# Sums of squares in four column tiles of TensorE, added by a copy and a second product

## The reference

```python
def rmsnorm(x, g):
    xf = x.astype(jnp.float32)
    xf = xf * lax.rsqrt(jnp.mean(xf * xf, axis=-1, keepdims=True) + EPS)
    return (xf * g.astype(jnp.float32)).astype(x.dtype)

mod = jax.nn.silu(cond) @ p['ada_w'][l] + p['ada_b'][l]
m = jnp.split(mod[:, None, :], 9, axis=-1)
h = rmsnorm(x, p['norm_pre'][l, n]) * (1 + m[3 * n + 1]) + m[3 * n]
y = sub_layer(h)
x = x + m[3 * n + 2] * rmsnorm(y, p['norm_post'][l, n])    # times 0.5 in the feed-forward blocks
```

## Time and profile before

| | us |
|---|---|
| median of 3 runs | 2387.17 |
| lowest and highest run | 2387.05, 2389.72 |
| profiled execution | 2387.35 |
| its span, first to last instruction | 2385.6 |
| TensorE busy | 2261.7 (95%) |
| VectorE busy | 957.6 (40%) |
| ScalarE busy | 902.6 (38%) |
| GpSimd busy | 1275.3 (53%) |
| mean granted clock of TensorE | 0.973 |

### The profile page before, as it was taken

The page is one execution under the profiler, slowest core; times in us unless marked ns, Lnnn a source line. Parts: engine busy times, 40 slices in busy tenths (PEclk is TensorE's granted clock), DMA queues, the critical chain, the costliest instruction groups (busy, mean ns, idle before and its releaser), DMA issues.

```text
span 2385.6 us, 33453 instructions
## 1 busy us (share of the span) xinstructions
PE 2261.7 (95%) x13833; PEld 2117.2 (89%) x13833; DVE 957.6 (40%) x1530; ACT 902.6 (38%) x1219; POOL 1275.3 (53%) x988
## 2 busy tenths in 40 slices
PE   7999999998999999999999999999898999899998
PEld 5999997996899897999979999799787999799997
DVE  4122115435778455222242111425366774631212
ACT  4222223344744454222342222323556544432231
POOL 2655553443488463666636566453334974456663
PEclk8999999998999999999999999999999999999998
DMA  8555754332222264445545556443222223534431
GB/s 264 177 177 177 229 168 141 107 89 61 72 67 79 81 202 133 144 140 170 177 138 150 161 161 214 128 141 95 68 76 69 71 84 114 157 98 128 129 120 67
DMA packets 362223, 311.47 MB, mean 131 GB/s; under 512 B 9923, under 2 KB 359383, under 8 KB 362071
## 3 DMA queue, kind: packets, MB, share of 16 engines
q1 hardware_dynamic: 354967, 303.55, 41.6%
q10 hardware_dynamic: 7104, 5.77, 0.8%
HBM read 305.35 MB, written 3.93 MB: 130 GB/s over the span
## 4 chain that ended last, share of the span: by engine, by line
PE 75%; DVE 10%; ACT 7%; issue 2%; DMA 2%; SPq 1%; POOL 1%; ACTq 0%; DVEq 0%
PE X L548 53%; PE S L548 8%; PE Ab L548 4%; PE X L813 2%; DMA raw<-in_ada_w 2%; ACT w_hi L992 1%; PE Ab L586 1%; PE S L586 1%; SPq L466 1%; PE S L597 1%; PE X L731 1%; PE S L760 1%; DVE x L1532 1%; DVE y L1530 1%; ACT p L1148 1%
## 5 line engine op out<-in xcount | busy, mean ns | idle before, releaser
L489 POOL TENSOR_TENSOR w_lo<-raw,w_hi 128x512 fp32r<-128x512 f32 (+1 forms) x872 | 1168.3, 1361 | 1056.3 <-ACT w_hi L992 1050.7
L992 ACT ACTIVATE w_hi<-raw 128x1024 fp32r<-128x1024 f32 (+1 forms) x436 | 453.0, 1041 | 768.3 <-PE X L548 732.8
L548 PE MATMUL X<-h_hi,w_hi 128*128 128x384 f32 x1600 | 546.2, 341 | 7.1 <-DVE h_lo L1485 7.1
L548 PE MATMUL X<-h_lo,w_hi 128*128 128x384 f32 x1600 | 539.4, 337 | 0.0
L548 PE MATMUL X<-h_hi,w_lo 128*128 128x384 f32 x1600 | 539.0, 337 | 0.0
L548 PEld LDWEIGHTS X<-h_hi,w_hi 128*128 128x128 f32 x1600 | 303.7, 190 | 29.0 <-issue 20.1
L548 PEld LDWEIGHTS X<-h_lo,w_hi 128*128 128x128 f32 x1600 | 303.8, 190 | 0.0
L548 PEld LDWEIGHTS X<-h_hi,w_lo 128*128 128x128 f32 x1600 | 303.5, 190 | 0.0
L1541 DVE TENSOR_TENSOR prod<-X,silu 128x768 f32<-128x768 f32 x44 | 42.1, 957 | 515.8 <-PE X L548 515.8
L548 PE MATMUL X<-act_hi,w_hi 128*128 128x384 f32 x704 | 237.0, 337 | 0.0
L548 PE MATMUL X<-act_hi,w_lo 128*128 128x384 f32 x704 | 235.5, 334 | 0.0
(11 more groups left out here) (338 smaller groups left out, 3333.0 us busy)
## 6 DMA issues: line engine op xcount, KB each, us to landing
raw<-in_w_in SPq DMA_DIRECT2D x124, 512.0 KB, 3.8
raw<-in_ffn_gate SPq DMA_DIRECT2D x88, 512.0 KB, 3.8
raw<-in_ffn_up SPq DMA_DIRECT2D x88, 512.0 KB, 3.8
raw<-in_ada_w SPq DMA_DIRECT2D x84, 512.0 KB, 3.6
raw<-in_ffn_down SPq DMA_DIRECT2D x80, 512.0 KB, 3.5
hold<-in_ada_w SPq DMA_DIRECT2D x29, 512.0 KB, 5.8
first_w<-in_ada_w SPq DMA_DIRECT2D x16, 512.0 KB, 8.9
raw<-in_w_out SPq DMA_DIRECT2D x16, 512.0 KB, 6.2
```

What stands on the lines that cost most here:

```text
L489: ins = nc.gpsimd.tensor_tensor(slot(w_lo, u)[:, part], raw_of(u)[:, part], slot(w_hi, u)[:, part], SUB)
L548: mm = nc.tensor.matmul(dst, w[:, k, m * 128:m * 128 + 128], r_, start=start and k + j == 0, stop=stop and k == u.nk - 1 and j == 2)
L992: A(slot(w_hi, u), raw_of(u), ACT.Copy).then_inc(hi_ready[u.split], 1)
```

## The change

In `x_sums` the stationary operand is cut to 32 columns of ones, so that a product fills only 32 rows of the bank. Tile k goes to rows 32 * (k % 4) and up; tiles 0 to 3 start these four sums and tiles 4 to 7 end them. ScalarE copies the bank into `part`, a tile of 128 x 384 in SBUF at the place of `y_sum`. TensorE multiplies `part` with the 128x128 block of ones into the bank X[0]; each of the four sums stands there 32 times, and the scale under the root is 1 / (32 * D) in place of 1 / D. The sums of y and their root are left as they are.

```diff
@@ -112,6 +112,8 @@
     y_sum, o = at("y_sum", [128, T], f32, o)
+
+    part, _ = at("part", [128, T], f32, o - T * 4)
@@ -684,11 +686,17 @@
             def x_sums(units):
                 for k in range(KT):
+                    rows_ = slice(32 * (k % 4), 32 * (k % 4) + 32)
                     pe.wait_ge(S["x_sq_ready"], seen.next("x_sq_ready"))
-                    mm = nc.tensor.matmul(S5[:, 0:T], ones, sq[:, k, :], start=k == 0, stop=k == KT - 1)
+                    mm = nc.tensor.matmul(S5[rows_, 0:T], ones[:, 0:32], sq[:, k, :], start=k < 4, stop=k >= 4,
+                                          tile_position=(0, 32 * (k % 4)))
                     if k % 2 and k // 2 < len(units):
                         ada_step(units[k // 2])
-                mm.then_inc(S["sum_ready"], 1)
+                mm.then_inc(S["part_ready"], 1)
+
+                pe.wait_ge(S["part_copied"], seen.next("part_copied"))
+                nc.tensor.matmul(X[0][:, 0, 0:T], ones, part[:, :], start=True, stop=True).then_inc(S["sum_ready"], 1)
@@ -1051,6 +1059,13 @@
+            def root_of_parts():
+
+                act.wait_ge(S["part_ready"], seen.next("part_ready"))
+                A(part[:, :], S5[:, 0:T], ACT.Copy).then_inc(S["part_copied"], 1)
+                act.wait_ge(S["sum_ready"], seen.next("sum_ready"))
+                A(root[:, :], X[0][:, 0, 0:T], ACT.Sqrt, bias=eps[:, 0:1], scale=1.0 / (32 * D)).then_inc(S["root_ready"], 1)
@@ -1071,7 +1086,7 @@
                 x_squares(2, KT)
-                root_of_sums()
+                root_of_parts()
                 ada_take(groups[1])
```

More of the change, by code:

```diff
@@ L237, in build @@
         names = ("const_in table_in mask_in rows_in lam_in_s lam_ready x_in xs_in rows_turned vec_ready c_ready c_zero x_turned x_copied x_ready "
-                 "x_sq_ready y_sq_ready y_added sum_ready root_ready norm_ready hh_ready h_ready silu_ready act_ready "
+                 "x_sq_ready y_sq_ready y_added sum_ready part_ready part_copied root_ready norm_ready hh_ready h_ready silu_ready act_ready "
                  "dve_step act_step half_done gate_ready gate_free sum_made mg_hi_ready ada_used ada_copied mod_turned mod_taken "
```

## The result

| | before | after |
|---|---|---|
| median, us | 2388.02 (7 runs) | 2395.16 (7 runs) |
| lowest and highest run | 2387.05, 2389.72 | 2392.35, 2398.42 |
| span of the profiled execution | 2385.6 | 2390.6 |
| mean granted clock | 0.973 | 0.973 |

The ratio is 1.0032, with a 95% interval of 1.0021 to 1.0044: 7.1 us slower by the medians, where 6.4 were forecast, and 5.0 to 10.5 by the interval. The profiled execution lies low among the runs of the changed kernel, so its span is only 5.0 us longer; what follows is read gap by gap, not from the two spans.

What follows compares the result with a forecast made beforehand. TensorE's product stream was taken to set the time, started in each gap by the end of the sums. 1.48 added less 0.19 saved, over five gaps, gave 2387.2 + 6.4 = 2393.6 us, range 2390.2 to 2400.0.

Steps and rivals of the forecast that it cites:

- What bounds it: Five gaps between sub-layers: delaying the end of the sums by d delays TensorE's product stream by d, five times.
- What goes: End of each gap's sums: tile 7's product no longer queues behind tile 6's, 0.95 us against 1.14, 0.19 saved.
- What is added: Each gap, after the sums: ScalarE wake-up 0.04, copy 0.49, hand-over 0.04, product with ones 0.91; 1.48 us, nothing over it.
- The sum: All five gaps: 1.48 - 0.19 = 1.29 us a gap, 6.45 us in all.
- The clock: Slow 1.2 GHz stretches in each gap: a later stream may meet the rise earlier or later, 3.4 us either way.
- The opening: Before the first gap: costs nothing, since the last units wait for first loads; without that cover 1.29 us more.
- Tiles in a row: Rival, the sums' column tiles: they run one after another, nothing saved, 7.4 us more, 2394.6 us; chance 0.12.
- Hidden in four gaps: Rival: four gaps hide the delay, for instance if the three loads don't move; only the fifth pays, 2388.5 us; chance 0.05.
- Clock kept: Rival, all five gaps: the later start keeps the clock up, winning 7.5 us against 6.4, about 2386 us; chance 0.03.
- The clock that falls at the sums: Rival, the gaps: 1.2 GHz comes ahead of the new product, 13.5 us in all, 2407 us; chance 0.08.

Runs made afterwards that it cites:

- the tiles alone: Changed kernel without the copy and second product, so the root takes the four partial sums as they stand: 2387.27 us, ratio 0.9995 to the kernel before.
- the late product: Changed kernel with the turn and four units ahead of the product that adds the parts, in four gaps: 2391.9 us, ratio 1.0013 to the kernel before.
- the changed kernel with early units: Changed kernel with units 8 to 11 of the four long gaps behind the sums' second product: 2369.84 us, ratio 0.9928 to the kernel before.
- the doubled kernel: Changed kernel with a second copy and a third product after the first pair: 2401.85 us, ratio 1.0055 to the kernel before.

## Why the prediction was right

**What bounds it.** The step that mattered was that the end of the sums carries the stream in all five gaps, in four of them through TensorE's queue and three loads, not through the root. Shown: delaying the root by 3.4 us behind the units cost 3.1 us in all; bringing the units forward by two steps won some 8 and 18 us though the root came later. In the fifth gap the root's path carries it: its stream starts 5.49 us after the root in both kernels.

**What goes.** Forecast 0.19 us a gap, measured 0.26 (1.14 to 0.88), shown at the root by the tiles alone. The term was 0.07 too small: tile 7's product took 0.83 us from its start at 370.30, where the forecast took the 0.91 of a full-width pair. The rule of the Trainium skill on weight loads ("TensorE: Matmul & The Clock Gate", Part 3), by which nothing would be saved, didn't hold here: tile 7's weights were loaded from 370.30 on, while tile 6's product was in work, and four products in the same row groups ran in 1.20 us.

**What is added.** Forecast 1.48, measured 1.50: the copy 0.49 to 0.50, the product 0.91, hand-overs of 0.04 to 0.06. Shown by undoing the tiles (1.50) and by doubling (1.49).

**The sum.** 1.24 x 5 = 6.2 us of chain, where 6.45 was forecast. The interval of 5.0 to 10.5 us holds this sum by itself and the next one too, so the whole time alone doesn't tell them apart; the gap-by-gap rows do.

**The clock.** This was left as a term without a sign, and in the fifth gap it has one. (The forecast's extremes of the slow stretch over a stream, 1.9 and 4.6 us, were read a little short: the stretches reach to 926.0 and 1557.4, which makes 2.3 and 4.9 and changes its 3.4 us by little.) From the stream's first to 41st instruction it took 8.64 to 8.80 us in seven profiles without copy and product (8.70 and 8.66 for the kernel before itself), and 9.44 to 9.71 in six with one copy and product there: some 0.95 us more, every time. The clock's rows say where it comes from. In the fifth gap the slow stretch lasts 6.8 us in all 14 profiles. It starts 3.3 to 3.5 us after the last square in the seven without copy and product, and 6.6 to 6.9 after it in the seven with them: the stretch moved by over 3 us while the stream moved by 1.24. So 5.5 us of it lie over the stream in place of 3.6, and at half clock the 1.9 more cost 0.95. It isn't a matter of more delay, more loss: with two copies and products the stretch starts where it does with one, but the stream starts 1.49 later, 4.3 us of the stretch lie over it, and the 40 instructions took 9.00. 6.2 + 0.95 = 7.15 agrees with the 7.1 measured, more closely than an interval this wide can show, so that closeness is luck in part. Why the stretch starts at these two places stays open. In the other four gaps the same span of 40 instructions moves by up to 1.4 us between the two profiles of the kernel before, so whether the change has a part there isn't settled by these runs. The two profiles of the changed kernel even spent less time in it there (33.9 and 32.8 us in four gaps) than the two of the kernel before (34.6 and 35.5), which is part of why their spans are low.

**The opening** cost nothing, shown by the change made there alone, within the interval of 2.1 us less to 1.9 more.

**The rivals.** Tiles in a row: refuted. Hidden in four gaps: refuted by the delayed chain in each of them. Clock kept: not seen after the change. The clock that falls at the sums: not in any gap, where it stays 1.00 through the sums, but it did happen in the opening, in the stretch from 20.6 to 24.0: in both profiles of this kernel, in one of two of the tiles alone and of the late product, and in the changed kernel with early units. The rows of the changed kernel in the opening and over its first gap's sums:

```profile
20.60:24.00 3.40, 3.40 (x28) 0.56 1.12 352
...
364.50:372.70 8.20, 6.02 (x21) 1.00 0.00 1
```

In the other profiles of kernels with tile sums in the opening (the second ones of those two, the doubled kernel, the opening alone) it stayed at 1.00 in that stretch. The fall cost nothing that can be seen: the last square of the first gap ends at 369.9 to 372.1 us in the five profiles with it, and at 371.2 to 371.8 in the four without.

## What to carry to other kernels

When a wait in one engine's queue is lengthened, ask what stands behind it in that queue before asking who needs the result: here the root had 4.5 to 5 microseconds to spare (its path starts the fifth gap's stream at 6.7 us, the others start at 11.2 to 11.7) and the units behind it had none, because loads waited for their buffers. Column tiles shorten a group of products only where they are ready together; where each waits for its own data, the win is the queueing of the last one, and a copy and a product to add the parts must cost less than that. Moving small work that releases buffers ahead of a wait for data won 18 us, and a third of that came from the clock, which in that profile no longer fell in the four gaps whose idle time had shrunk.

## What the runs showed of the hardware

- Four column-tile products of 384 columns in f32, with the same 128 rows and different moving data, took 1.20 us together, the last of them begun when its data came; four at full width took 3.02.
- A fixed idle time left a repeatable mark: in the fifth gap the first 40 instructions of the stream took 8.64 to 8.73 us in five profiles of four kernels that have the same instructions there, although the gap lies at different times of each execution. Where the idle time ends with a load, the same figure moved by up to 1.5 us between two profiles of one kernel.
- Work added ahead of an idle time moved the slow stretch by more than the work lasts: in the fifth gap 1.24 us more moved its start by over 3 us, and 2.73 us more moved it no further.
- The third of three 512 KB loads took 6.1 to 6.7 us in two profiles of the kernel before, which issues them within 1 us, and 4.4 to 5.8 in the one profile in which they were issued 2 us apart.
- A load of 512 KB in the chain of the four gaps took between 6.1 and 7.2 us in two profiles of one kernel, with the same issue time to 0.02 us after the last square. Together with the clock this may be what spreads the changed kernel's runs over 6 us; only two of its executions have a trace, so it isn't shown.
- In the opening the granted clock fell to 1.2 GHz at 20.6 to 21.2 us in five of nine profiles of kernels with column-tile sums there, and in none of five with full-width sums. From 17.2 to 20.6 TensorE was busy for 2.3 to 2.6 us with tile sums, whether the clock then fell or not, and for 3.1 to 3.2 at full width. What decides between the two stays open.
